# A transformer block and a two-layer gated block on one core: the next group's first split in front of the evacuation, the gates' sigmoid in pairs

## The reference, cut to what matters

```python
ya = dilated_mixture_attention(...) @ w_branch_a      # 512 -> 2048
yb = stick_breaking_attention(...) @ w_branch_b       # 512 -> 2048
gate_a, gate_b = sigmoid(gla), sigmoid(glb)           # 256 x 2048 each
mix = (gate_a * ya + gate_b * yb) @ w_out
h = h + rmsnorm(mix, g_mix_post)
u = rmsnorm(h, g_ffn_pre)
up = causal_depthwise_conv(u @ w_up, conv_w, conv_b)  # 2048 -> 2 x 5632, three taps along the tokens
gate_ff, value = split(up)
f = (gelu(gate_ff) * value) @ w_down                  # 5632 -> 2048
```

## Time and profile before

| | |
|---|---|
| three runs | 3408.97, 3414.98, 3415.59 us, median 3414.98 |
| the profiled execution | 3413.3 us, span 3411.5 us, mean granted clock 0.988 |
| TensorE busy | 3292.8 us (97%) |
| VectorE, ScalarE, GpSimd busy | 1537.0 (45%), 1419.3 (42%), 32.7 us (1%) |
| DMA | 556.97 MB, mean 163 GB/s; highest slice of 85 us (595 to 680) 256 GB/s |
| branches | about 522 to 579 us of the span |
| output projection | about 579 to 671 us |
| up projection | about 689 to 1245 us |

### The profile page before, as it was taken

How to read it: one execution, slowest core, us unless ns; L and a number is a source line. 1 busy time by engine, 2 the same in 40 slices (tenths; PEclk the granted TensorE clock), 3 DMA queues, 4 the chain that set the end, 5 groups by cost and what they waited for, 6 DMA issues and landing times.

```text
span 3411.5 us, 48332 instructions
## 1 busy us (share of the span) xinstructions
PE 3292.8 (97%) x20802; PEld 2859.4 (84%) x20802; DVE 1537.0 (45%) x1951; ACT 1419.3 (42%) x1962; POOL 32.7 (1%) x30
## 2 busy tenths in 40 slices
PE   7999998999999999999999999999799999999998
PEld 7989998689999987777777778788689888888886
DVE  5444445555555554446232222342544455453554
ACT  5444544544444444447321122232654444444443
POOL 0000002000000000000000000000000000000000
PEclk9999999999999999999999999999899999999999
DMA  6665544756666666665455555443423233232343
GB/s 207 184 189 174 153 151 157 256 189 227 220 225 206 216 227 246 230 231 185 144 173 169 172 171 170 154 141 101 131 81 105 88 102 108 92 106 91 101 136 118
DMA packets 349060, 556.97 MB, mean 163 GB/s; under 512 B 16880, under 2 KB 148976, under 8 KB 347696
## 3 DMA queue, kind: packets, MB, share of 16 engines
q1 hardware_dynamic: 346304, 540.08, 48.7%
q0 software_dynamic: 2256, 13.11, 1.0%
q10 hardware_dynamic: 288, 0.70, 0.1%
HBM read 551.60 MB, written 2.23 MB: 162 GB/s over the span
## 4 chain that ended last, share of the span: by engine, by line
PE 54%; ACT 5%; DVE 4%; issue 2%; DMA 0%; DVEq 0%; ACTq 0%
PE ps L675 48%; PE ps L700 2%; ACT whi L1049 1%; PE ps L868 1%; PE ps L890 1%; ACT hA L1224 1%; PE ps L872 1%; DVE hA L1804 1%; PE ps L886 1%; ACT L1224 1%; DVE hA L1796 1%; DVE wlo L1568 0%; DVE hB L1793 0%; DVE hB L1791 0%; PE ps L731 0%
## 5 line engine op out<-in xcount | busy, mean ns | idle before, releaser
L1568 DVE TENSOR_TENSOR wlo<-raw,whi 128x1024 fp32r<-128x1024 f32 x819 | 999.7, 1228 | 1503.5 <-ACT whi L1049 1496.0
L1049 ACT ACTIVATE whi<-raw 128x1024 fp32r<-128x1024 f32 x824 | 861.8, 1058 | 1395.7 <-PE ps L675 710.6
L675 PE MATMUL ps<-HCh,whi 128*128 128x512 f32 (+1 forms) x1664 | 606.3, 364 | 2.1 <-DVE HCl L1639 2.1
L675 PE MATMUL ps<-HCl,whi 128*128 128x512 f32 (+1 forms) x1664 | 595.3, 358 | 0.0
L675 PE MATMUL ps<-HCh,wlo 128*128 128x512 f32 (+1 forms) x1664 | 595.0, 358 | 0.0
L675 PE MATMUL ps<-Vh,whi 128*128 128x256 f32 x1408 | 403.6, 287 | 12.9 <-DVE wlo L1568 12.8
L675 PE MATMUL ps<-Vh,wlo 128*128 128x256 f32 x1408 | 398.2, 283 | 0.0
L675 PE MATMUL ps<-Vl,whi 128*128 128x256 f32 x1408 | 398.2, 283 | 0.0
L675 PE MATMUL ps<-whi,HCh 128*128 128x256 f32 (+1 forms) x1152 | 377.2, 327 | 1.6 <-DVE HCl L1666 1.5
L675 PEld LDWEIGHTS ps<-HCh,whi 128*128 128x128 f32 x1664 | 316.3, 190 | 71.2 <-issue 21.6
L675 PE MATMUL ps<-wlo,HCh 128*128 128x256 f32 (+1 forms) x1152 | 368.3, 320 | 0.0
(11 more groups left out here) (301 smaller groups left out, 4088.5 us busy)
## 6 DMA issues: line engine op xcount, KB each, us to landing
raw<-in_ada_w SPq DMA_DIRECT2D x192, 512.0 KB, 5.7
raw<-in_w_up SPq DMA_DIRECT2D x176, 512.0 KB, 5.1
raw<-in_w_in SPq DMA_DIRECT2D x160, 512.0 KB, 3.7
raw<-in_od_w_in SPq DMA_DIRECT2D x160, 512.0 KB, 3.5
raw<-in_ev_w_in SPq DMA_DIRECT2D x96, 512.0 KB, 6.2
raw<-in_w_down SPq DMA_DIRECT2D x88, 512.0 KB, 5.1
raw<-in_w_out SPq DMA_DIRECT2D x32, 512.0 KB, 5.2
raw<-in_w_ple_gate SPq DMA_DIRECT2D x32, 512.0 KB, 3.8
```

Of the source, the lines that this page charges most:

```text
L675: mm = e.matmul(o, a, b, start=first and t == 0, stop=last, skip_group_check=True)
L1049: e.activation(m.whi[ch.i % SPLIT][:, 0:n], m.raw[ch.slot][:, 0:n], ACT.Copy).then_inc(S("hi"), 1)
L1568: e.tensor_tensor(m.wlo[ch.i % SPLIT][:, 0:n], m.raw[ch.slot][:, 0:n], m.whi[ch.i % SPLIT][:, 0:n].bitcast(F32), ALU.subtract).then_inc(S( ...
```

## The change

A group's walk now remembers the last chunk whose splits were made (`made`, `upto`), so that the splits placed at a group's first chunk can be made earlier than its walk begins (`early`). In the up projection ScalarE and VectorE do so before the evacuation of the group in front, `down0` included. In the branches ScalarE makes the first turn's early split, then two pieces of the sigmoid (the gates of group `ba` and of group `bb` of this turn), and so in each turn; VectorE waits for two more pieces in each turn instead of for all eight in the first.

```diff
@@ class Engine
-        self.beside, self.serial = [], False
+        self.beside, self.serial, self.made = [], False, -1
@@ def chunks
-            self.splits(ch.c)
+            self.upto(ch.c)
             self.pump()
...
+    def upto(self, c):
+
+        if c > self.made:
+            self.made = c
+            self.splits(c)
+
+    def early(self, name):
+
+        self.upto(self.plan.by[name].chunks[0].c)
@@ def scalar, branches
-    for i in range(8):
-        e.activation(m.gt[:, 4 * i:4 * i + 4, :], m.gt[:, 4 * i:4 * i + 4, :], ACT.Sigmoid).then_inc(S("gt_sig"), 1)
-    for g in range(4):
+    for g in range(4):
+        P.early(f"ba{g}")
+        for i in (g, g + 4):
+            e.activation(m.gt[:, 4 * i:4 * i + 4, :], m.gt[:, 4 * i:4 * i + 4, :], ACT.Sigmoid).then_inc(S("gt_sig"), 1)
         P.chunks(f"ba{g}")
@@ def scalar and def vector, up projection
             G = P.chunks(f"up{2 * g + half}", V, 3)
+            P.early(f"up{2 * g + half + 1}" if g + half < 11 else "down0")
@@ def vector, branches
-        if g == 0:
-            e.wait_ge(S("gt_sig"), 8)
+        e.wait_ge(S("gt_sig"), 2 * g + 2)
```

## The result

The changed kernel takes 3422.03 us (median of 12 runs, 3416.03 to 3431.12), the kernel before on the same chips 3415.60 (12 runs, 3408.97 to 3417.66). The ratio is 1.0023, 95% interval 1.0013 to 1.0032: slower by 8 us, between 4 and 11 (the two medians alone lie 6.4 apart).

A forecast was written before the change was run, and what follows sets the result against it. TensorE, busy 97%, bounds the kernel; only its idle and half-clock time can be won. Terms -3.4 - 0.6 + 9.9 + 2.3 - 5.6 + 0.7 = +3.3 on 3413.3 gave 3417, own range 3411 to 3423, overall 3407 to 3427.

The forecast's parts named there:

- slower by over 0.2%: Whole kernel: outcome slower than before by more than 0.2% (6.8 us); chance 0.27.
- Late landings behind five even groups: Up projection, behind groups 2, 6, 10, 14, 18: moved splits wait for late data, TensorE idles; 9.9 us lost (8 to 16).
- side estimate: Up projection loads: a 512 KB transfer takes 3.2 us by the skill's fit, making the loss 5.6 without a halved clock.
- Odd groups: Up projection, ten idle stretches behind odd groups: low part leaves the chain, landing wait enters; together -0.6 us (-3 to +3).
- Start of `down0`: Start of the down projection: idle 1.0 instead of 3.75 us and clock stays up; gain 5.6 us, low end 2.75.
- Branches: Branches: sigmoids in four pairs and earlier splits start `out0` sooner; gain 3.4 us, low end 1.7.
- The walk: Branches: step-by-step timing of chunks, splits and sums, giving `ba2` at 550.1, `ba3` at 562.3, `out0` at 575.75.
- Clock: TensorE's clock halved behind new idle stretches: +2.3 us behind the 3.2 us one, +0.7 behind one near 2.4.
- rival B: Some eight idle stretches (four even boundaries, four odd, two branches) each halve the clock, 1.5 us apiece: +15, 3428; chance 0.20.
- Rival A: Up projection: late data land early enough for the fifth chunk, only gains stay: -9.6, 3404; chance 0.12.
- Rival C: Output projection: waits for its weights and gives the branch gain back: 3420; chance 0.08.
- Rival D: Up projection: the move does nothing, both halves come to less than 2 us, 3413 to 3416; chance 0.06.

The follow-up runs named there:

- e3: Up-projection early splits alone against the kernel before, with the old order kept behind groups 2, 6, 10, 14, 18; -4 us (-7 to -1).
- e5: Kernel before plus the early split behind groups 2, 6, 10, 14, 18 alone; +17 us (12 to 22).
- e9: As e3, but behind groups 2, 6, 10, 14, 18 ScalarE's split stands between evacuation and gelu, VectorE's behind its taps; -3 us (-6 to 0) against the kernel before.
- e2: Kernel before plus the early splits of the up projection alone, down0 included, branches as before; +12 us (7 to 16).
- e4: Kernel before plus the early split at the start of down0 alone; -2 us (-5 to +1).
- e1: Kernel before plus the branch half alone (sigmoid in pairs, the turns' early splits), up projection as before; -2 us (-5 to +1).
- e10: The changed kernel again, unaltered, for a second series and second profile; ratio to the kernel before 1.0028 (1.0018 to 1.0038).
- e7: Changed kernel without early up-projection splits, sigmoids from the second pair on placed before ScalarE's wait for the mixture's sum; -6 us (-10 to -3) against the kernel before.
- e6: Kernel before with the product of the two sides one chunk later (a yield on ScalarE and VectorE), no early splits; -13 us (-17 to -9).

## Why the prediction was right, and which term was too small

The forecast was 3417 with its own range of 3411 to 3423; measured 3422.0. The mechanism is the one forecast, the size is two to three times the +3.3 of the sum: it was +8 and +10 in the two series, and the interval of neither holds 3.3. That 3422.0 still lies in the range, by 1 us, is in part luck. Of the 5 us between 3417 and 3422, 2.3 are the base: the sum started from the profiled execution (3413.3), and the kernel before has a median of 3415.6. The chances were less well placed than the range: +0.23% is just over the line of 0.2%, and "slower by over 0.2%" had been given 0.27. Point by point:

- **Late landings behind five even groups, +9.9: right.** 1.80, 1.77, 3.20, 1.70, 1.85, together 10.3 (second profile 9.0), with evacuations 5.7 to 7.2 us after the group's end. e3, e5 and e9 show it by experiment. That three boundaries have nothing to move, and that the even ones with data in time cost nothing, came as said. The prediction's side estimate, 3.2 us for a load, rests on a fit that the Trainium skill (DMA: Bandwidth & Descriptors, Anatomy of one DMA) gives for DMAs issued by GpSimd. These are SyncE's, and of the 227 loads into raw buffers from 690 to 1250 in the kernel before none took under 3.5 us (median 5.3).
- **Odd groups, -0.6: right within its ends.** 13.4 us in place of 12.8, in the second profile 12.3. The move does nothing for this chain unless the data are there: behind `up5` and `up13` the stretch is 0.22, behind `up7` 2.75. The outlier is `up19`, 2.64 for a forecast of 1.4 (second profile 1.48); in e2's profile it is 4.08.
- **Start of `down0`, -5.6: about right.** The stretch from there is shorter by 4.8 (e4: 5.1). Idle 0.8 to 1.4, clock up.
- **Branches, -3.4: about 0.5 too large.** Stage 56.9 to 55.3, 54.0 and 52.6 in three profiles, e1 -2 in the runs. In all three the idle time is the same, 5.6 instead of 6.7; what differs is the clock, halved twice, once and not at all. With it halved once, as the forecast had it, the gain is 2.9 (e1). The walk had one price too low. It took 1.85 us for a VectorE split beside a GpSimd split, from a row (549.41) of which GpSimd's covers only 0.77 us; where it covers more, the same trace of before has 2.85 and 2.62:

```profile
535.71 2.67 POOL L553 TENSOR_TENSOR wlo<-raw,whi 128x1024 fp32r<-128x1024 f32 x1 [13.63 <-ACT whi L1049]
```

```profile
536.61 2.85 DVE L1568 TENSOR_TENSOR wlo<-raw,whi 128x1024 fp32r<-128x1024 f32 x1 [0.49 <-ACT whi L1049]
...
561.48 2.62 DVE L1568 TENSOR_TENSOR wlo<-raw,whi 128x1024 fp32r<-128x1024 f32 x1 [0.74 <-ACT whi L1049]
```

In the changed kernel, before `ba2`, the first of VectorE's two splits runs beside GpSimd's and takes 2.58, the second does not and takes 1.21. `ba2` stands idle for 2.72, where the walk had 2.45 (550.1 - 547.65):

```profile
545.23 2.41 POOL L563 TENSOR_TENSOR wlo<-raw,whi 128x1024 fp32r<-128x1024 f32 x1 [4.96 <-ACT whi L1059]
```

```profile
546.14 2.58 DVE L1580 TENSOR_TENSOR wlo<-raw,whi 128x1024 fp32r<-128x1024 f32 x1 [2.25 <-ACT whi L1059]
```

```profile
548.64 1.21 DVE L1580 TENSOR_TENSOR wlo<-raw,whi 128x1024 fp32r<-128x1024 f32 x1
```

- **Clock, +2.3 and +0.7: the mis-sized term.** The forecast let one stretch of 3.2 us halve it and put the other new ones, 1.6 to 2.4, nearly all on the safe side; that was kept for rival B. In the first profile it was halved behind 1.80, 2.75, 3.20 and 2.64, each for 3.4 us, 4 x 1.7 = 6.8 lost, and in the branches behind 2.72 and 2.0. In the second profile once in the up projection and not in the branches, less than forecast. So the profiles lie on both sides, and what holds for the runs is read from their granted clocks: span times (1 - clock) is the time lost to it, and its mean in the series with e10 is 44.9 us for the changed kernel (9 executions) and 40.4 for the kernel before (19); the twelve of the first series have 44.2. That is +4.4 us of clock in a mean difference of +9.5. The forecast's clock terms were +3.0 for new stretches less 4.3 for the two that go (2.8 at `down0`, 1.5 in the branches), -1.3 together. The difference, near 6, is about what the sum lacked in this series (9.5 - 3.3). It is an estimate: each clock is given to three digits (0.001 is 3.4 us), and half clock while TensorE waits is counted though it costs nothing.

Rival B was half right: stretches near 1.8 can do it, not all of them, and not each time. Its +15 counted eight such stretches where its own list has ten, which would be +18; with the clock as it was, neither came. Rival A (landings hidden) fell with the landings of 3.8 and 5.2. Rival C: the output projection has no idle stretch of note in any profile (0.4 to 0.7 us near its end in some), and from `out0` to `up0` it is 108.9 to 111.8 us in the five profiles with new branches, 108.9 to 111.0 in the seven with those of before. e7's 5.5 us of branches come out as 6 in the runs, so nothing was given back. Rival D fell with e3 and e5.

Open: the runs put e5 at +17, its profile shows 9.2 of idle time behind the five groups. Its granted clocks, read as above, add 5.2 us against the kernel before, 14.4 together, where the means of the times lie 15.7 apart; the rest of 1.3 was not traced. How often the clock falls behind a given stretch was not counted, since only one or two executions of each kernel have a trace. That GpSimd's splits slow VectorE's is seen in rows, in each of the profiles, but was not taken away by an experiment. Why `up19`'s stretch varies from 1.48 to 4.08 between executions is open too.

## What to carry to other kernels

Work that is moved forward in an in-order queue takes its own waits with it. Before putting a load-fed step in front of an evacuation, read when its data land, boundary by boundary, and ask what else then stands behind that wait; e9 moved the same split by one step less and lost nothing. Where TensorE is short of a split, look for the instruction in front of it that waits for another engine (ACh, MIXh), and fill that wait with the split instead: a `yield`, a reordered loop and the one early split whose data were there gave 22 us, the change lost 8.

## What the runs showed of the hardware

The twelve executions of the changed kernel range over 15 us, and the granted clock goes along: the longest (3431.12) has a mean of 0.985, the shortest (3416.03) 0.989. A share of 0.004 of 3420 us is 13.7 us of the 15.1 (each share is rounded to 0.001, that is 3.4 us).

Whether an idle stretch of TensorE is followed by half clock is not settled by its length. In front of the first branch matmul there is the same stretch of 2.10 us in all twelve profiles: behind it the clock was at 1.2 GHz for 3.4 us in ten and stayed at 2.4 GHz in two (e6, and the changed kernel's second profile, whose program is that of the first). In the changed kernel's first profile 1.80 us was followed by half clock (783.4), 1.85 was not (1199.89). Between the first branch matmul and `down0`, not counting the waits for weights in front of `up0`, no stretch under 1.80 us was followed by half clock in any profile, the 1.3 us behind the odd groups of before among them. The price of an idle stretch near 2 us is thus itself plus 0 or 1.7 us.

A VectorE split of 128x1024 takes 1.23 us alone and 2.6 to 3.0 where a GpSimd split runs beside most of it. Where VectorE's starts second, the extra time is 0.8 to 0.9 of the overlap: 1.62 us more for an overlap of 1.77 at 536.61 in the kernel before, 1.35 for 1.50 at 546.14 in the changed one. Where it starts first and its last 0.1 to 0.55 us overlap, it takes 1.21 to 1.23 all the same. GpSimd's own split took 2.4 to 2.8.
